# Hybrid attention block: token-major projection and norm of queries and keys, and sixteen conditioning slices moved from TensorE to VectorE, ScalarE and GpSimd

## What is computed

```python
mx = split((silu(c) @ ada_w[i] + ada_b[i]), 6)           # shift, scale, gate, twice; the same with c_ctx
hx = rms_norm(xs, norm_mix[i]) * (1 + mx[1]) + mx[0]     # latent tokens; context tokens with mc
q, k, v = split(h @ w_qkv, 3)                            # h of latent and of context tokens
q = head_rms_norm(split_heads(q, 16), q_gain)            # over the 64 features of a head
k = head_rms_norm(split_heads(k, 16), k_gain)
y = softmax(q @ k.T * scale + bias) @ v
xs = xs + mx[2] * (merge_heads(y) @ w_o)
```

## Time and profile before

| | us |
|---|---|
| median of 3 runs | 2459.2 (2458.76 to 2459.67) |
| span of the profiled execution | 2459.5 |
| PE busy | 2401.0 (98%) |
| DVE busy | 1795.9 (73%) |
| ACT busy | 1020.3 (41%) |
| POOL busy | 639.5 (26%) |

### The profile page before, as it was taken

How to read it: one execution, slowest core, us unless ns; L and a number is a source line. 1 busy time by engine, 2 the same in 40 slices (tenths; PEclk the granted TensorE clock), 3 DMA queues, 4 the chain that set the end, 5 groups by cost and what they waited for, 6 DMA issues and landing times. The chain is left out here.

```text
span 2459.5 us, 36114 instructions
## 1 busy us (share of the span) xinstructions
PE 2401.0 (98%) x12656; PEld 1970.3 (80%) x12656; DVE 1795.9 (73%) x2614; ACT 1020.3 (41%) x1545; POOL 639.5 (26%) x442
## 2 busy tenths in 40 slices
PE   8998899999999999999999999999999999999999
PEld 5775588888888878888888887668888888867999
DVE  4877569888974355437888777988988777855874
ACT  4336534443232244414444324554444324355543
POOL 3314333332300020032333224843333225001000
PEclk9999999999999999999999999999999999999999
DMA  8551025555633321233554543523554545312556
GB/s 310 172 169 52 18 86 172 176 172 196 218 107 101 107 75 52 94 97 136 178 171 165 185 158 119 150 79 137 171 175 160 190 158 138 112 43 72 192 181 189
DMA packets 104681, 346.29 MB, mean 141 GB/s; under 512 B 13248, under 2 KB 22912, under 8 KB 104576
## 3 DMA queue, kind: packets, MB, share of 16 engines
q1 hardware_dynamic: 74960, 248.65, 30.3%
q10 hardware_dynamic: 26352, 86.77, 10.9%
q0 software_dynamic: 3264, 9.44, 1.8%
HBM read 335.02 MB, written 1.05 MB: 137 GB/s over the span
## 5 line engine op out<-in xcount | busy, mean ns | idle before, releaser
L752 PE MATMUL bank<-Hhi,Whi 128*128 128x512 f32 (+1 forms) x2416 | 866.7, 359 | 20.2 <-DVE Hlo L1748 7.5
L754 PE MATMUL bank<-Hhi,Wlo 128*128 128x512 f32 (+1 forms) x2416 | 852.9, 353 | 0.0
L753 PE MATMUL bank<-Hlo,Whi 128*128 128x512 f32 (+1 forms) x2416 | 852.7, 353 | 0.0
L1661 DVE TENSOR_TENSOR Wlo<-raw,Whi 128x1024 fp32r<-128x1024 f32 x424 | 638.9, 1507 | 232.0 <-ACT Whi L1278 212.5
L1278 ACT ACTIVATE Whi<-raw 128x1024 fp32r<-128x1024 f32 x424 | 448.5, 1059 | 779.8 <-DMA raw<-in_weights 701.6
L752 PEld LDWEIGHTS bank<-Hhi,Whi 128*128 128x128 f32 x2416 | 456.8, 189 | 101.1 <-issue 22.4
L753 PEld LDWEIGHTS bank<-Hlo,Whi 128*128 128x128 f32 x2416 | 457.1, 189 | 63.8 <-issue 2.9
L754 PEld LDWEIGHTS bank<-Hhi,Wlo 128*128 128x128 f32 x2416 | 456.9, 189 | 62.3
L615 POOL TENSOR_TENSOR cond_w<-cond_w,cond 128x1024 f32<-128x1024 f32 x107 | 259.1, 2421 | 602.6 <-DVE square L1685 514.9
L752 PE MATMUL bank<-Ghi,Whi 128*128 128x512 f32 (+1 forms) x770 | 269.3, 350 | 0.0
L754 PE MATMUL bank<-Ghi,Wlo 128*128 128x512 f32 (+1 forms) x770 | 267.3, 347 | 0.0
(11 more groups left out here) (278 smaller groups left out, 2875.6 us busy)
## 6 DMA issues: line engine op xcount, KB each, us to landing
raw<-in_weights SPq DMA_DIRECT2D x424, 512.0 KB, 3.4
cond_w<-in_ada ACTq DMA_DIRECT2D x160, 512.0 KB, 4.0
ada_raw<-in_ada SPq DMA_DIRECT2D x16, 512.0 KB, 15.8
ada_ring<-in_ada SPq DMA_DIRECT2D x16, 512.0 KB, 6.7
rel_in<-in_rpb POOLq DMA_DIRECT2D x48, 128.0 KB, 4.7
shifted<-U SPq DMA_DIRECT2D x84, 66.0 KB, 2.1
decay_t<-in_dist POOLq DMA_DIRECT2D x4, 640.0 KB, 4.2
X<-in_x SPq DMA_DIRECT2D x4, 512.0 KB, 6.1
```

What stands on the lines that cost most here:

```text
L752: t.matmul(dst, Whi[:, st.slot, w], hi, start=start, stop=False)
L753: t.matmul(dst, Whi[:, st.slot, w], lo, start=False, stop=False)
L754: return t.matmul(dst, Wlo[:, st.slot, w], hi, start=False, stop=stop)
L1661: v.tensor_tensor(Wlo[:, st.slot, :], raw[:, st.slot, :], Whi[:, st.slot, :].bitcast(F32), ALU.subtract)\
```

## The change

- Keys and queries are projected as the values were: the tokens stand still, 512 weight columns move. `y` = 0, 1 are the two halves of the keys, 2, 3 of the queries, 4, 5 of the values; each takes 8 chunks `k` times 4 token blocks times 3 matmuls, into banks 0 to 3 and 4 to 7 by turns (`QKV_BANKS`). In layer 3, `y` = 2, 3 have two token blocks.
- After the last chunk of `y` ACT squares the banks, DVE sums the squares per head along the free axis (`head_root`, 8 values per token and block), ACT takes one root, DVE one reciprocal of 128 x 32, and DVE multiplies each bank by the inverse into `qk_rows`. `head_sum` is gone.
- PE transposes `qk_rows` back into the banks of `y` (`turned_rows`, 16 transposes, 8 for two blocks) after chunk 4 of `y + 1` (chunk 6 where `y + 1` has two blocks); ACT multiplies by the gain into `QK` (`placed`). `y + 2` waits for `placed(y)`.
- In layer 3, `by_streams` interleaves `y` = 0 with the norm of the layer's input, and three weight groups instead of two are split during that norm.
- `ada_slice`, `ada_cols` and `ada_ring` are gone. Their 16 groups become slots of the conditioning ring: layer 0 hosts 24 slots beside `y` = 1 to 5, by the table `HOSTED[y][quarter]`. The first two are not shared, the other 22 are. The head stage hosts none. POOL scales slots 2 and 3 ahead of the second half of `rel`.
- At the start SP interleaves four conditioning pieces and four weight groups one to one.

```diff
-ADA_START = 4
 FIRST_SLICES = 4
-ADA_QK = 4
-ADA_FIRST = ADA_START + ADA_QK
+ADA_FIRST = FIRST_SLICES
 QUAD = P // 4
 COND_SLOTS = 3
 PER_LAP = 3
-IN_V = 8
+HOSTED = ((0, 0, 0, 0), (0, 1, 0, 1), (1, 1, 1, 2), (2, 1, 1, 2), (2, 1, 1, 2), (2, 1, 1, 1))
+IN_MIX = sum(map(sum, HOSTED))
+ALONE = sum(HOSTED[1])
 V_LATE = 2
 LATE_SPLITS = (5, 9)
-IN_HEADS = 0
-IN_O = ()
...
+QKV_BANKS = (0, 1, 2, 3), (4, 5, 6, 7)
...
-            return n < IN_V + IN_HEADS or any(p["hosts"] and p["cond_up"] <= n < p["cond_down"] for p in layers)
+            return ALONE <= n < IN_MIX or any(p["hosts"] and p["cond_up"] <= n < p["cond_down"] for p in layers)
...
+        def hosted_in(y, quarter):
+            first = sum(map(sum, HOSTED[:y])) + sum(HOSTED[y][:quarter])
+            return range(first, first + HOSTED[y][quarter])
+        def qkv_blocks(layer, y):
+            return (2, 3) if layer == DEPTH - 1 and y in (2, 3) else (0, 1, 2, 3)
...
+                    if half and layer == 0:
+                        pool.wait_ge(cond_ready, 2)
+                        for n in range(ALONE, ALONE + 2):
+                            scale_weights(n)
...
-                    pool.wait_ge(cond_ready, 2)
-                    for n in range(IN_V):
+                    for n in range(ALONE + 2, IN_MIX):
                         scale_weights(n)
...
-                def head_sum(k_static, k, tok):
-                    pe.wait_ge(qk_squared, qk0 + k + 1)
-                    t.matmul(bank[4 + k_static % 2][:, tok], one_head[:, :], na_sq[:, k_static % 2, tok],
-                             start=True, stop=True).then_inc(qk_summed, 1)
...
-                            ada_slice(0)
-                            head_sum(2, 2, tok)
-                            ada_cols(ADA_START)
...
+                def chunk_products(y, k, blocks):
+                    st = Step(p["mix"] + 4 * y + k // 2)
+                    for b in blocks:
+                        tk = slice(P * b, P * b + P)
+                        last = three_moving(bank[QKV_BANKS[y % 2][b]][:, :], st, slice(512 * (k % 2), 512 * (k % 2) + 512),
+                                            Hhi[:, k, tk], Hlo[:, k, tk], k == 0, k == C - 1)
+                    return last
+                def turned_rows(y):
+                    pe.wait_ge(tile_free, FREE0 + tile0 + TB * (y + 1))
+                    for c in range(4):
+                        for b in qkv_blocks(layer, y):
+                            last = t.transpose(bank[QKV_BANKS[y % 2][c]][:, P * b:P * b + P],
+                                               qk_rows[:, b, P * c:P * c + P], ident[:, :])
+                        last.then_inc(qk_turned, 1)
...
+                def by_streams():
+                    pe.wait_ge(tile_free, tile0 + 2)
+                    for k in range(C):
+                        if k % 2 == 0:
+                            pe.wait_ge(lo_split, p["mix"] + k // 2 + 1)
+                        pe.wait_ge(h_ready, p["mix_ready"] + k + 1)
+                        chunk_products(0, k, (0, 1))
+                        if k == 4:
+                            norm_sum(2 * layer, XT)
+                        if k == 6:
+                            norm_spread(2 * layer, XT)
+                    pe.wait_ge(tile_free, tile0 + 4)
+                    for k in range(C):
+                        pe.wait_ge(h_ready, p["mix_ready"] + C + k + 1)
+                        last = chunk_products(0, k, (2, 3))
+                        if k % 2:
+                            last.then_inc(weights_used, 1)
...
+                for y in range(1, 6):
+                    blocks = qkv_blocks(layer, y)
+                    if y >= 2:
+                        pe.wait_ge(qk_placed, 4 * (4 * j + y - 1))
+                    for k in range(C):
+                        if k % 2 == 0:
+                            pe.wait_ge(lo_split, p["mix"] + 4 * y + k // 2 + 1)
+                        last = chunk_products(y, k, blocks)
+                        if k % 2:
+                            last.then_inc(weights_used, 1)
+                        if k == (4 if len(blocks) == TB else 6) and y <= 4:
+                            turned_rows(y - 1)
...
-                def root_of(k_static, k, tok):
-                    act.wait_ge(qk_summed, qk0 + k + 1)
-                    a.activation(na_root[:, k_static % 4, tok], bank[4 + k_static % 2][:, tok], ACT.Sqrt,
-                                 bias=eps[:, :], scale=1.0 / NA_HD).then_inc(qk_root, 1)
+                def squares(y):
+                    act.wait_ge(weights_used, p["mix"] + 4 * y + 4)
+                    for nth, b in enumerate(qkv_blocks(layer, y), qk_blocks_before(layer, y)):
+                        if nth >= 2:
+                            act.wait_ge(qk_summed, nth - 1)
+                        a.activation(na_sq[:, nth % 2, :], bank[QKV_BANKS[y % 2][b]][:, :], ACT.Square)\
+                            .then_inc(qk_squared, 1)
+                def roots(y):
+                    act.wait_ge(qk_summed, qk_blocks_before(layer, y + 1))
+                    b0 = qkv_blocks(layer, y)[0]
+                    a.activation(head_root[:, b0:, :], head_root[:, b0:, :], ACT.Sqrt, bias=eps[:, :], scale=1.0 / NA_HD)\
+                        .then_inc(qk_root, 1)
+                def placed(y):
+                    part = 1 - y // 2
+                    tok = XT if len(qkv_blocks(layer, y)) == 2 else ALL
+                    for c in range(4):
+                        act.wait_ge(qk_turned, 4 * (4 * j + y) + c + 1)
+                        a.activation(QK[:, C * part + 4 * (y % 2) + c, tok], bank[QKV_BANKS[y % 2][c]][:, tok], ACT.Copy,
+                                     scale=qk_gain[:, j, part:part + 1]).then_inc(qk_placed, 1)
...
+                def hosts(y, quarter):
+                    if layer == 0:
+                        for n in hosted_in(y, quarter):
+                            if n > ALONE:
+                                sum_products(n - 1)
+                            if n:
+                                reload(n - 1, p["cond_end"])
...
+                for y in range(4):
+                    squares(y)
+                    roots(y)
+                    if y == 3:
+                        a.preload_act_table(ACT.Exp)
+                    for quarter in range(4):
+                        split(Step(p["mix"] + 4 * (y + 1) + quarter))
+                        hosts(y + 1, quarter)
+                        if quarter == (1 if len(qkv_blocks(layer, y + 1)) == TB else 2):
+                            placed(y)
+                act.wait_ge(rel_ready, 2 * j + 2)
+                evict_v(0)
+                for quarter in range(4):
+                    if quarter < 4 - late:
+                        split(Step(p["v"] + 4 + quarter))
+                    hosts(5, quarter)
...
+                    sum_products(IN_MIX - 1)
+                    reload(IN_MIX - 1, p["cond_end"])
+                evict_v(1)
...
-                    def normed(m, k, i, tok):
-                        dve.wait_ge(qk_root, qk0 + k + 1)
-                        v.reciprocal(na_root[:, m, tok], na_root[:, m, tok]).then_inc(qk_rstd, 1)
-                        dve.wait_ge(qk_rstd, qk0 + k + 1)
-                        v.scalar_tensor_tensor(QK[:, C * part + m + 4 * i, tok], bank[m][:, tok],
-                                               qk_gain[:, j, part:part + 1],
-                                               na_root[:, m, tok], ALU.mult, ALU.mult).then_inc(tile_free, 1)
...
+                def normed_rows(y):
+                    blocks = qkv_blocks(layer, y)
+                    for nth, b in enumerate(blocks, qk_blocks_before(layer, y)):
+                        dve.wait_ge(qk_squared, nth + 1)
+                        v.tensor_reduce(head_root[:, b, :], by_heads(na_sq[:, nth % 2, :]), axis=AX, op=ALU.add)\
+                            .then_inc(qk_summed, 1)
+                    dve.wait_ge(qk_root, 4 * j + y + 1)
+                    roots = head_root[:, blocks[0]:, :]
+                    v.reciprocal(roots, roots).then_inc(qk_rstd, 1)
+                    dve.wait_ge(qk_rstd, 4 * j + y + 1)
+                    dve.wait_ge(qk_turned, 4 * (4 * j + y))
+                    for b in blocks:
+                        v.tensor_tensor(by_heads(qk_rows[:, b, :]), by_heads(bank[QKV_BANKS[y % 2][b]][:, :]),
+                                        head_root[:, b, :].unsqueeze(2).to_broadcast([P, 512 // NA_HD, NA_HD]), ALU.mult)\
+                            .then_inc(tile_free, TB // len(blocks))
...
+                for y in range(4):
+                    normed_rows(y)
+                    for quarter in range(4):
+                        split(Step(p["mix"] + 4 * (y + 1) + quarter))
+                        hosts(y + 1, quarter)
                 dve.wait_ge(rel_ready, 2 * j + 2)
-                late = V_LATE if layer == 0 else 0
                 v.memset(rel_flat[:, 0:CTX], 0.0).then_inc(biased, 1)
```

(28 more changed lines are left out.)

237 lines of the change are left out of this document (54 added, 183 removed).

## The result

The changed kernel takes 2471.62 us (median; 2470.3 to 2471.97), the kernel before on the same chip 2459.41 us: a ratio of 1.0043, with a 95% interval of 1.0031 to 1.0054. So it is slower, by 0.43%. The prediction said 2461 us, within 0.2% of the kernel before, as the likeliest, with a range up to 2471, which the median misses by 0.6 us. The profiled execution spans 2470.0 us, 10.5 more than before.

What follows compares the result with a forecast made beforehand. TensorE, 98% busy, looked like the bound, but VectorE and GpSimd share a port beside layer 0's values. 2459.5 + 12.9 (layer 0) + 1.7 (clock) - 12.5 (layer 3) = 2461.6 us by span, 2461 by median; range 2447 to 2471.

Steps and rivals of the forecast that it cites:

- The port: Layer 0: VectorE's splits, stores, weighings and GpSimd's work take turns at one resource; second head step 12.9 us later.
- The prices: Layer 0, per y: reductions 0.65 us, products 0.62 us each on DVE, at no port time.
- Even perfectly packed, layer 0 gains nothing: Layer 0: shared port work without a gap ends at 197 us; the second head step began at 193.8.
- The clock: Layer 0: TensorE's granted clock falls during 15 us of waiting; 1.7 us of work lost, taken once.
- the slower rival: Layer 0: clock falls to 1.2 GHz at each wait, 3.4 us lost each time; 2469 us, chance 0.20.
- Layer 3: Keys and queries: 85.6 us fall to 73.1, a gain of 12.5 us.
- kept for the range: Layer 3: a wait for weights, asked for faster beside the queries, was left out of the 73.1 us.
- The spacing: Stages between layer 0 and layer 3: the forecast sum has no term for them.
- same: Whole kernel: within 0.2% (4.9 us) of 2459.2 us; chance 0.37.
- the forecast case: Whole kernel: 2461 us with an error of 5 us, likeliest 2456 to 2466; chance 0.52.
- Packed port: Layer 0: DVE and POOL trade order better, the gaps don't happen, cost 1 to 3 us; 2449 us, chance 0.22.
- TensorE bounds: Layer 0: exclusion lifted or port time hidden, queries and values run at TensorE's pace; 2427 us, chance 0.06.

Runs made afterwards that it cites:

- e4: Changed kernel with every conditioning slot of layer 0's mixer weighed on VectorE, none scaled by GpSimd and summed by ScalarE: 2447.1 us, ratio 0.9941.
- e9: Changed kernel without layer 3's relative biases: GpSimd clears the table with one memset, neither loads nor adds: 2468.4 us, ratio 1.0026.
- e1: Changed kernel with 384 unused bytes per partition, so the big shared region starts where it did in the kernel before: 2466.0 us, ratio 1.0019.
- e3: Kernel before with only 16 unused bytes per partition added, which move the region by 32: 2470.9 us, ratio 1.0042.
- e2: Changed kernel with 16 unused bytes per partition added, which move the region by 32: 2476.8 us, ratio 1.0065.
- e6: Changed kernel with slots weighed by VectorE alone and 36 floats of padding, which move the region by 160 bytes: 2453.1 us, ratio 0.9972.

## Why the prediction was right or wrong

- **The port, right.** The forecast had the transposes of `y` = 2 wait for 8.4 us and those of `y` = 3 for 5.4; they waited for 9.10 and 5.08. The values were to end at 189.6 and ended at 190.3; the second head step was to be 12.9 us late and was 12.2. The port held for 102.1 of 115.2 us shows the cause, and e4 bears it out: with less port time per slot and more VectorE time the waits shrink.
- **The prices.** Four reductions in a row take 2.63 us and four products 2.48, so 0.66 and 0.62 us each (taken: 0.65 and 0.62). Two reductions beside a scaling (149.9) and nine beside additions of `rel` took 0.67 to 0.69 us, and five products beside such additions 0.68 to 0.69, as the others do alone. So to cost them at no port time was right. 16 transposes take 1.91 us, 0.12 each.
- **"Even perfectly packed, layer 0 gains nothing": right for shared slots, and the wrong question.** The prediction itself worked out 27 us less of the port for slots kept on VectorE; e4's port is held for 24 us less. The Trainium skill (Perfetto Trace Analysis, Optimizing Scalar/DVE Operations) warns that moving work between VectorE and GpSimd might not help. The runs agree: e4 is 24 us shorter by taking work back from GpSimd.
- **The clock, a small miss.** It fell to 1.2 GHz after each of the three waits of layer 0 began (from 119.6, 153.7 and 194.7, for 10.2, 6.8 and 17.1 us; the granted clock of 190.3 to 206.0 is 0.64). The transposes behind the two waits took 3.68 us instead of 1.91, but the next stage was late on VectorE anyway. Only 1.0 us of it is left behind the second head step (+12.2 there, +13.2 at the end of the heads), where 1.7 was taken. So the slower rival had the falls of the clock right and their price wrong: 3.4 us each for two of them, of which nothing shows at the second head step. That its 2469 us is the nearest number is luck.
- **Layer 3, the first failed step.** The prediction kept 1.2 of the 8.3 us of norm matmuls and waits and came to 73.1 us, a gain of 12.5, with a wait for a load "kept for the range". From start to values it took 77.1, gain 8.5 by that stretch and 7.5 up to the heads. The waits were mis-sized: the bias loads and additions beside the weights of `y` = 1 and 3 cost 3.9 us (e9); the other 1.1 us up to the heads stay open. By the prediction's own test, "if layer 3 gains less than 10", it was wrong here. I had priced `rel` on the port in layer 0, and forgot it in layer 3.
- **The spacing, the second.** Code that the change doesn't touch was costed at nothing. It cost 5.8 us up to layer 3 (of 6.3 that were added there), more than the whole bound of "same", because small tensors ahead of the region changed size (e1, e3). Without it the changed kernel would have been at +0.19% (e1), just inside the forecast case. Against the forecast of 2461.6 us by the span, the port is 0.7 us under, the clock 0.7 under, layer 3 5.0 over, the spacing with what lies beside it 6.3 over and the rest behind layer 3's heads 1.5 under: 8.4 us in all.
- **"Packed port" and "TensorE bounds"** had 0.28 together. POOL waited 8.41 and 7.17 us for VectorE across the two norms (before the scalings at 126.84 and 158.33), so the gaps that I had drawn do exist; and nothing lifted the exclusion: the port was held for 102.1 us where 108.5 had been added up.

## What to carry to other kernels

Before work is moved beside TensorE, add up what each engine pair takes of a resource that they share, per stage, and compare it with TensorE's time there; splitting one job over VectorE and GpSimd can cost more of that resource than leaving it on one. When an allocation ahead of big operands changes size, look at the start-to-start distance of the matmuls in stages that the change doesn't touch, and try a few bytes of padding: here 384 unused bytes were worth 0.24%. Read the addresses from the built program: adding up the sizes of the tensors gave wrong ones here, and three of the edits (e2, e3, e6) didn't test what they were meant to. A gain on the bound engine should be read in a stage only after asking what loads and helpers run beside it at the new pace.

## What was not expected of the hardware

The distance between fp32r matmuls at 2.4 GHz depends on where the moving operand lies in SBUF: for 512 columns 226.7 ns for `Hhi` and `Hlo`, and 228.9 or 233.3 ns for the tensors of the region, moved by 32 to 384 bytes; for 256 columns 113.9, 117.8, 118.2 or 119.9 ns. The means of 461 pairs agree within 0.1 ns in each of three layers. Positions 256 bytes apart agreed in both pairs tried. Next to that, a store of 128 x 2 values took 0.15 us free and 2.35 us (at 172.99) when GpSimd held the port.
